# Hybrid decoder trunk on one Trainium2 core: list spans and zero pad made by GpSimd, rank tests ahead of the first gated product, places product in the rounded kind

## The reference, cut to what matters

```
t = rms_norm(x, norm_ffn[l]).reshape(512, 1024)
g_idx = argmax(t @ w_group + b_group);  g_w = softmax(...)[g_idx]
top_p, top_i = top_k(softmax(expert logits of that group), 2);  top_p /= sum(top_p)
for each of 32 experts e, over the tokens that chose it:
    y = (silu(xb @ w_gate[e]) * (xb @ w_up[e])) @ w_down[e]
    out[token] += y * g_w * top_p
```

## Time and profile before

| what | us |
|---|---|
| median of 3 runs | 1148.9 (1148.19 to 1148.99) |
| the profiled execution's own time | 1148.85 |
| its span, first to last instruction | 1147.0 |
| PE busy | 1103.0 (96%) |
| DVE busy | 672.4 (59%) |
| ACT busy | 372.9 (33%) |
| POOL busy | 67.5 (6%) |
| granted PE clock, mean | 0.987 |

### The profile page before, as it was taken

One profiled execution on the slowest core, in us unless ns is written; L12 is line 12 of the kernel. 1 busy time (PEld: TensorE's weight loads), 2 busy tenths in 40 slices (PEclk: granted clock), 3 DMA queues, 4 the chain that ended last, 5 costly groups with the idle time before them and its releaser, 6 DMA issues.

```text
span 1147.0 us, 16734 instructions
## 1 busy us (share of the span) xinstructions
PE 1103.0 (96%) x4876; PEld 600.0 (52%) x4876; DVE 672.4 (59%) x1580; ACT 372.9 (33%) x811; POOL 67.5 (6%) x123
## 2 busy tenths in 40 slices
PE   7999999999799999999999999999997999999997
PEld 4854555556574444444457545555566544444443
DVE  4236765467685555555652477655667755555554
ACT  5226331114433333333252263210243433333332
POOL 1000000000007000000000000000000250000001
PEclk9999999999889999999999999999997999999999
DMA  9031024500319999999641300245005299999992
GB/s 351 2 109 39 1 74 147 220 1 1 151 73 406 417 421 421 423 422 422 263 157 44 103 1 1 75 147 220 1 2 220 108 404 422 421 423 422 421 422 105
DMA packets 50925, 243.20 MB, mean 212 GB/s; under 512 B 6512, under 2 KB 16784, under 8 KB 25520
## 3 DMA queue, kind: packets, MB, share of 16 engines
q1 hardware_dynamic: 50048, 240.78, 52.6%
q0 software_dynamic: 384, 1.31, 0.3%
q10 hardware_dynamic: 432, 0.38, 0.1%
HBM read 240.36 MB, written 2.10 MB: 211 GB/s over the span
## 4 chain that ended last, share of the span: by engine, by line
PE 85%; DVE 7%; ACT 2%; issue 2%; DMA 1%; DVEq 1%; ACTq 0%; POOLq 0%; SPq 0%
PE ps L2756 19%; PE ps L2300 12%; PE ps L2782 10%; PE ps L2564 9%; PE ps L2290 7%; PE ps L2717 6%; PE ps L2718 5%; PE ps L2268 5%; PE ps L2612 2%; PE ps L2383 2%; PE ps L2327 2%; DMA X<-in_x 1%; PE ps L2422 1%; PE ps L2619 1%; DVE xlo L2013 1%
## 5 line engine op out<-in xcount | busy, mean ns | idle before, releaser
L2756 PE MATMUL ps<-wgu,xw 128*64 128x512 f32 x1024 | 225.2, 592 | 0.2
L2127 DVE TENSOR_TENSOR X<-ps,X 128x512 f32<-128x512 f32 x253 | 154.5, 682 | 6.9 <-issue 6.1
L2300 PE MATMUL ps<-hT,ring 128*128 128x512 f32 x352 | 156.8, 595 | 0.0
L2756 PEld LDWEIGHTS ps<-wgu,xw 128*64 128x64 f32 x1024 | 73.5, 137 | 145.7 <-issue 144.0
L2782 PE MATMUL ps<-wdn,hhT 128*64 128x512 f32 x512 | 116.9, 598 | 0.0
L974 ACT ACTIVATE xw<-xgT 128x512 f32 (+1 forms) x132 | 81.9, 624 | 107.3 <-issue 92.9
L2564 PE MATMUL ps<-ring,yT 128*128 128x512 f32 x256 | 115.0, 596 | 0.9 <-DVE ssqY L1798 0.8
L2717 PE MATMUL ps<-yhi,Wt 128*128 128x512 f32 x256 | 106.6, 416 | 0.2
L2300 PEld LDWEIGHTS ps<-hT,ring 128*128 128x128 f32 x352 | 64.6, 190 | 69.8 <-issue 69.8
L2718 PE MATMUL ps<-ylo,Wt 128*128 128x512 f32 x256 | 100.9, 394 | 0.0
L2148 DVE SCALAR_TENSOR_TENSOR ylo<-ps,ws,yhi 128x512 fp32r<-128x512 f32 x64 | 48.1, 751 | 63.8 <-ACTq L1370 63.3
(11 more groups left out here) (364 smaller groups left out, 1344.5 us busy)
## 6 DMA issues: line engine op xcount, KB each, us to landing
wgu<-in_w_gate SPq DMA_DIRECT2D x64, 1024.0 KB, 10.3
wgu<-in_w_up SPq DMA_DIRECT2D x64, 1024.0 KB, 12.4
wdn<-in_w_down SPq DMA_DIRECT2D x64, 1024.0 KB, 12.6
ring<-in_w_in SPq DMA_DIRECT2D x8, 1024.0 KB, 6.6
ring<-in_w_mix_out SPq DMA_DIRECT2D x12, 512.0 KB, 6.3
w_kv<-in_xa_w_kv SPq DMA_DIRECT2D x4, 1024.0 KB, 8.5
ring<-in_w_in SPq DMA_DIRECT2D x2, 2048.0 KB, 15.5
ring<-in_w_in SPq DMA_DIRECT2D x2, 1536.0 KB, 14.0
```

Source lines behind the costliest of these rows:

```text
L2127: tt(xh, bank, xh, ALU.add).then_inc(mfreed((what, n)), 1)
L2300: last = mm(bank, w[:, c, c0:c0 + P], hT[:, c, :], start=c == 0, stop=c == KD - 1)
L2756: last = mm(bank[r], xw[:, c, j, 0:SLOTS], wgu[2 * parity + j][:, :, c, :], start=c == 0, stop=c == KD - 1)
```

## The change: what it does

`list_spans` becomes a function of POOL, called as soon as ACT has kept the ranks (`rank_kept`); the zero pad follows it there, and `spans_ready` then stands for both. DVE waits for `spans_ready` ahead of `tiles_past`. `ranks_shown` and `params_free` move from behind `hh` to the end of the preparation, ahead of `step_(0, ...)`. `diag` and `all_ones` get the rounded kind; `all_ones` is written by a multiply-add on DVE in place of a memset. Two drains are added on DVE.

```diff
--- before.py
+++ after.py
@@ -492,7 +492,7 @@
         pos_i = at("pos_i", [P, NT], I32, o + 10240)
         freqs = at("freqs", [P, 16], F32, o + 10304)
         rt = at("rt", [P, 16, NT * NE], F32, o + 8192)
-        all_ones = rt[:, 5]
+        all_ones = at("all_ones", [P, P], F32R, o + 8192 + 5 * 4 * NT * NE)
         spans = rt[:, 15, 0:3 * NE].bitcast(I32)
         passed = rt[:, 9:13].rearrange("p a (b e) -> p (a b) e", e=NE)
         o += 16384
@@ -502,7 +502,7 @@
         late += KD * SORTED * 4
         xhi = at("xhi", [P, NT, D], F32R, late)
         yhi = at("yhi", [P, 2, D], F32R, late)
-        diag = at("diag", [P, 2 * NT, P], F32, late + 4096)
+        diag = at("diag", [P, 2 * NT, P], F32R, late + 4096)
         ranked = at("ranked", [P, 2 * NT, P], F32, late + 12288)
         ylo = at("ylo", [P, 2, D], F32R, late + 8192)
         late += 16384
@@ -897,6 +897,16 @@
                 pool.drain()
                 summed(dst)
 
+            def list_spans():
+
+                n_lists = HALVES * NE
+                second_rank = rt[:, 0].rearrange("p (t e) -> p t e", t=NT)[:, NT // HALVES:NT]
+                combined(rt[:, 1, 2 * NE:3 * NE], row(1), rt[:, 1, NE:2 * NE], ALU.add)
+                combined(second_rank, second_rank, row(1).unsqueeze(1).to_broadcast([P, NT // HALVES, NE]), ALU.add)
+                scaled(rt[:, 4, n_lists:n_lists + NE], row(1), float(SLOTS), None, ALU.min)
+                pool.drain()
+                nc.gpsimd.tensor_copy(spans, rt[:, 4, 0:3 * NE])
+
             def overflow_table():
 
                 combined(ovf_f[:, 1:2], ovf_f[:, 1:2], ovf_f[:, 0:1], ALU.add)
@@ -957,6 +967,12 @@
                 for t in range(2, NT):
                     wait_apart(pool, S["sqO_ready"], done(l, "sqO_ready", NT + t + 1))
                     joined(sqM, slice(t * P, (t + 1) * P), "sqM_joined")
+
+                wait_apart(pool, S["rank_kept"], done(l, "rank_kept", 1))
+                list_spans()
+                pool.memset(xgT[:, :, 2 * SEQ:SORTED], 0.0)
+                pool.drain()
+                pool.nop().then_inc(S["spans_ready"], 1)
                 wait_apart(pool, S["params_free"], l + 2)
                 overflow_table()
                 if l == DEPTH - 1:
@@ -2004,7 +2020,7 @@
                 tt(rt[:, 5].rearrange(by_half, g=HALVES, e=NE), ranked_from,
                    lists.unsqueeze(2).to_broadcast([P, HALVES, NT // HALVES, NE]), ALU.add)
                 signal("rank_read")
-                rank, first_count, counts = r32(0), row(1), rt[:, 1, 2 * NE:3 * NE]
+                rank, counts = r32(0), rt[:, 1, 2 * NE:3 * NE]
                 chosen(dest, r32(5), slice(0, NT // HALVES))
 
                 def low_part(t):
@@ -2023,16 +2039,6 @@
                     dve.drain()
                     stt(hot, iota[:], place[:, 1, t:t + 1], hot.bitcast(F32), ALU.is_equal, ALU.add)
                     signal("G_ready")
-
-                def list_spans():
-
-                    dve.wait_ge(S["rank_kept"], done(l, "rank_kept", 1))
-                    ts(rt[:, 4, n_lists:n_lists + NE], first_count, float(SLOTS), None, ALU.min)
-                    tt(counts, first_count, rt[:, 1, NE:2 * NE], ALU.add)
-                    tt(rank[:, 2:4], rank[:, 2:4], first_count.unsqueeze(1).to_broadcast([P, 2, NE]), ALU.add)
-                    dve.drain()
-                    nc.vector.tensor_copy(spans, rt[:, 4, 0:3 * NE])
-                    signal("spans_ready")
 
                 def sorted_gain(half):
                     for c in range(1, KD, 2):
@@ -2089,7 +2095,7 @@
                     shape = [P, 2 * NT, P]
                     tt(diag[:], ident[:].unsqueeze(1).to_broadcast(shape),
                        flat(srel).unsqueeze(2).to_broadcast(shape), ALU.mult)
-                    nc.vector.memset(all_ones, 1.0)
+                    ts(all_ones[:], iota[:, 0:P], 0.0, 1.0, ALU.mult, ALU.add)
                     nc.vector.tensor_copy(slot[:], slot_0[:])
                     signal("place_ready")
 
@@ -2136,8 +2142,6 @@
                     if back:
                         bring_back(p, "comb", range(8))
                     else:
-                        ranks_shown()
-                        signal("params_free")
                         slot_weights()
                         dve.wait_ge(S["places_ready"], done(l, "places_ready", 2))
                         spread(parity)
@@ -2155,19 +2159,22 @@
                 low_part(1)
                 chosen(dest, r32(5), slice(NT // HALVES, NT))
                 ts(dest_2[:], dest[:], -float(SEQ), None, ALU.add)
-                list_spans()
+                dve.drain()
                 one_hot(2)
                 low_part(2)
-                nc.vector.memset(xgT[:, :, 2 * SEQ:SORTED], 0.0)
                 sorted_gain(0)
                 low_part(3)
                 one_hot(3)
+                dve.wait_ge(S["spans_ready"], done(l, "spans_ready", 1))
                 tiles_past()
+                dve.drain()
                 sorted_gain(1)
                 padded_places()
                 placed()
                 chosen(rank_k, rank)
                 token_weights()
+                ranks_shown()
+                signal("params_free")
                 step_(0, 0, False)
                 with dve.Fori(0, PAIRS // 2 - 1) as i:
                     for k in range(2):
@@ -2726,7 +2733,7 @@
                     pe.wait_ge(S["place_ready"], done(l, "place_ready", 1))
                     for k in range(2):
                         bank = mbank_of(l, 0, ("places", k))
-                        mm(bank, all_ones, diag[:, NT * k:NT * (k + 1), :], start=True, stop=True
+                        mm(bank, all_ones[:], diag[:, NT * k:NT * (k + 1), :], start=True, stop=True
                            ).then_inc(mfilled(("places", k)), 1)
 
                 def slot_weights():
```

## The result

The changed kernel is slower. Its median is 1151.97 us over 22 runs (1149.31 to 1154.95), against 1149.03 before (22 runs, 1148.19 to 1150.53); the ratio is 1.0024, 95% interval 1.0016 to 1.0031. Its runs also spread over 5.6 us, where those of before spread over 2.3. The profiled execution took 1151.06, with a span of 1149.2. The forecast was 1147.6, with a range of 1146.4 to 1151.2.

A forecast was written before the change was run, and what follows sets the result against it. The prediction took PE to bound the kernel, except where PE waits for DVE. From 1148.85 it took (0.75 - 0.1) for layer 0 and (0.7 - 0.1) for layer 1, giving 1147.6, range 1146.4 to 1151.2.

The forecast's parts named there:

- rival 4: At `tiles_past`, DVE waits for POOL; this needs POOL to take 16 us for 2.2 of work; chance nothing.
- Rival 3: POOL and DVE block each other at the top bound, 0.6 of each layer's 0.7 gone: 1148.6, no change; chance 0.10.
- rival 2: At `hh`, DVE does not decide: its chain shrinks or SiLU bounds; 2.55 gained a layer, 1143.8; chance 0.07.
- the new hole: PE's idling of 1.8 us from 342.03, between gate and up and the transposes, where the places product stood before.
- One layer's fall: The clock falls in the stretch behind gate and up in one layer, costing 2.5 us: 1150.1; chance 0.25.
- Both: The clock falls there in both layers, 2.5 us each: 1152.6, slower than before; chance 0.08.
- The rival's sum for two falls: Rival of a clock fall behind gate and up: 1147.6 with 2.5 us lost in each layer, 1152.6; chance 0.08.

The follow-up runs named there:

- POOL's part alone: The changed kernel with plain f32 places and the rank tests back behind `hh`, so list spans and pad on POOL; 1147.83 us, ratio 0.9987 against the kernel before.
- the three repeated executions: The changed kernel run three times more, unchanged, one profiled execution each: 1149.60, 1152.76 and 1153.32 us.
- the covered kernel: The changed kernel with each rounded places product written four times into the same bank; 1148.39 us, ratio 0.9995 against the kernel before.
- the rank tests alone: The kernel before with only the rank tests moved ahead of the first `hh`; median 1149.07 us, ratio 1.0 against the kernel before.
- the rounded product alone: The kernel before with only the places product (`diag`, `all_ones`) in the rounded kind; 1155.02 us, ratio 1.0047 against the kernel before.
- the rank tests back: The changed kernel with the rank tests put back behind `hh`, rounded places kept; 1152.57 us, ratio 1.0031 against the kernel before.

## Why the prediction was wrong

The critical path was right step by step in layer 0, and in layer 1 up to the token weights. DVE's first copies end 1.01 us ahead (14.99 behind the rank product in place of 16.00; 1.08 said); gate and up start 0.85 and 0.82 earlier (0.92); `hh` starts at +31.35 where +31.26 was said, after the tests and not after SiLU; PE idles 1.62 and 1.96 us (1.8); `slot_weights` starts 0.69 and 0.33 earlier (0.75 and 0.7), so layer 1 gives half of what was said. Without a fall pair 1 comes 0.76 and 0.42 earlier, 1.2 in all where the sum had 1.25; that the total is so near is luck in part, as layer 0 gives more than its 0.65 and layer 1 less than its 0.6. POOL beside DVE costs 0.06 a layer (0.1 taken, 0.6 the bound). DVE waits for POOL nowhere, so rival 4 is out. Rival 3 is out with POOL's part alone, which gains, and rival 2 with `hh`'s row.

The step that failed is that the sum has no term for the clock: it puts a fall in the new hole at nothing, on the strength of one row, and gives falls a third of the chances ("One layer's fall: 0.25. Both: 0.08."). In four profiles of the changed kernel the clock fell in 6 of 8 layers, and in every one of them at least once. The evidence that I set against it was ill chosen. In the row from 22 to 29 us PE was busy 4.72 of 7 us at 1.00, but idling was all that it shared with the new hole. The case that was like it is the one that the prediction names beside it, the router of layer 1, in the trace of before:

```profile
870.21 2.87 PE L2619 MATMUL ps<-packed,hT 128*128 128x36 f32 x16 [0.38 <-ACT lg L974]
...
870.50:871.00 0.50, 0.50 (x7) 0.50 (x6) 0.35 (x3) 0.00 (x0) 0.00 (x0) 1.00 0.54 229
871.00:871.50 0.50, 0.50 (x5) 0.50 (x4) 0.35 (x3) 0.00 (x0) 0.00 (x0) 0.52 1.09 459
```

Here the clock fell at 871 while PE was busy with 36-column products, with 0.38 us of idling ahead of them; from 868 to 871 PE was busy 2.62 of 3 us. `slot_weights` is 16 products of 32 columns. From this row I conclude that for the clock the hole did not end with the transposes but with the down products; no run changed `slot_weights`, so that its narrow products share in the fall is argued and not shown. What is shown is that PE's 512-column products ahead of the transposes matter: taken away alone it costs 6.0 us, and given back it returns them. The prediction says that "instructions issued do not hold it up" and then counts the hole against a row that was busy with wide work.

The price failed too, by a smaller part: 2.5 a fall was said with bounds of 1.3 and 3.5, and it came as 1.6 to 1.7 or as 3.3. The rival's sum for two falls, 1152.6, is near the profiles with two (1152.8 and 1153.3), but by luck: in each of them a dear fall and a cheap one (3.3 and 1.7) came together, which make twice 2.5.

The Trainium skill ("TensorE: Matmul & The Clock Gate", section "HAM oscillation — how this bites in real kernels") was cited for an engine that idles between bursts and is throttled again. The trace agrees that the next burst runs slow, 0.50 from 346 to 352, but behind 1.62 us of idling, a shorter wait than the one that the section tells of. The Trainium skill (the same title, section "Part 1: The HAM clock gate (the "warmup" mystery)") says that the point at which the gate acts varies with the run, of the rise of the clock in sustained work; the variation between runs that the prediction gives under the other section stands here. Of the fall the three repeated executions show the same, in another set of layers or of another size each time.

The whole difference, from the medians: with the hole filled by the plain product, the changed kernel's other parts give 1147.86 - 1149.05 = -1.2. POOL's part alone has the same median gain, and 1.6 by its trace, of which the rank tests ahead of `hh` take 0.4. The falls cost 1151.97 - 1147.86 = 4.1 (3.6 against the covered kernel); the four profiles lost 3.7 on average. Together that is the +2.9 measured. The shorter places product gives nothing, since `hh` and the rank tests end later than it.

The kernels with plain or covered places still had single runs at 1149.9 to 1150.9, 3 to 4 us over their fastest, where POOL's part alone had none over 1148.62. That need not be a rarer fall in the hole: the kernel before spreads as far (1148.08 to 1151.37), and the one such run with a profile, the rank tests alone at 1150.34, had lost its time ahead of the sort.

Open: why the rounded product alone lost more (6.0, both layers at 3.3 in its profile) than the changed kernel with the longer single pause (4.1), and what decides between a fall and none in layers with the same pauses.

## What to carry to other kernels

A product that PE executes while it waits anyway is not waste to be trimmed: here 1.3 us of it less in each layer, off the critical path, cost 6.0 us, and writing it four times brought all of it back. When an edit takes work off PE in front of a wait, add up the whole stretch until dense products run again, narrow products included as the router's row suggests, and compare it with the stretch of the same trace in which the clock fell, not with one that merely idled. Where a kernel's time spreads more after an edit than before it (5.6 us here, against 2.3 to 3.3 in the sets of runs of before), look at the granted clock of several executions before looking for a slower instruction.

## What the runs showed of the hardware that I had not expected

- A lost stretch comes in two sizes: pair 1 was late by 1.63, 1.67 and 1.71 us, or by 3.28, 3.30 and 3.33, in the changed kernel. The three falls in the kernels with the rounded product alone and with the rank tests back were of the dear kind, 3.28 to 3.32.
- In all six kernels with spans on POOL, and in no other, DVE stands still for 0.42 or 0.43 us in layer 1 among the token weights, waiting for nothing that the trace shows. After the change it is here, and it is what takes 0.36 from layer 1's gain in the changed kernel:

```profile
909.63 0.18 DVE L2086 RECIPROCAL wk<-rt 128x4 f32<-128x4 f32 x1
910.23 0.16 DVE L2088 TENSOR_TENSOR wk<-wk,rt 128x4 f32<-128x4 f32 x1 [0.43 <-issue]
```

With the rank tests behind `hh`, the wait for SiLU hides most of it (POOL's part alone gives 0.83 and 0.76). What causes it was not tried.
